# Hymba decoder layer: first weights on the scalar queue, four split buffers, four-quarter openings, later squares on GpSimd

## The reference

```python
u = rms_norm(h, norm_mix);  z = u @ w_in                 # 1024 x 3328
y = concat(rwkv7_time_mix(z[:, :1792]), moba_attention(z[:, 1792:]))
h = h + y @ w_mix_out                                    # 1024 x 1024
h = h + softmax_attention(rms_norm(h) @ w_xq, rms_norm(mem) @ w_xkv) @ w_xo
h = h + square(relu(rms_norm(h) @ w_ff1)) @ w_ff2        # 1024 x 4096 x 1024
out = rms_norm(h, norm_final)
```

## Time and profile before

| | |
|---|---|
| median of 3 runs | 481.69 us (479.34, 481.69, 481.86) |
| profiled execution | 479.82 us, span 477.7 us |
| PE busy | 452.7 us, 95% |
| PEld busy | 404.3 us, 85% |
| DVE busy | 321.8 us, 67% |
| ACT busy | 246.5 us, 52% |
| POOL busy | 35.2 us, 7% |
| from HBM | 71.35 MB, 152 GB/s over the span |

### The profile page before, as it was taken

How to read it: one execution, slowest core, us unless ns; L and a number is a source line. 1 busy time by engine, 2 the same in 40 slices (tenths; PEclk the granted TensorE clock), 3 DMA queues, 4 the chain that set the end, 5 groups by cost and what they waited for, 6 DMA issues and landing times.

```text
span 477.7 us, 10346 instructions
## 1 busy us (share of the span) xinstructions
PE 452.7 (95%) x4390; PEld 404.3 (85%) x4390; DVE 321.8 (67%) x475; ACT 246.5 (52%) x396; POOL 35.2 (7%) x54
## 2 busy tenths in 40 slices
PE   4999999999899999899999997999999999999995
PEld 3999999878788888899998995888888888888883
DVE  3667899985567948569476367575747575666656
ACT  4799944245464446337344344555544354544444
POOL 8300000000000000052000053000000000000000
PEclk9999999999999999999999999999999999999999
DMA  8953464222422415454443155446565746657412
GB/s 247 308 186 114 151 195 149 92 92 80 124 93 89 126 59 170 137 171 159 153 155 111 50 144 160 157 140 231 177 196 161 245 151 217 199 197 230 142 69 88
DMA packets 59937, 73.05 MB, mean 153 GB/s; under 512 B 1378, under 2 KB 48564, under 8 KB 59892
## 3 DMA queue, kind: packets, MB, share of 16 engines
q1 hardware_dynamic: 59812, 72.14, 46.7%
q0 software_dynamic: 80, 0.26, 0.2%
HBM read 71.35 MB, written 1.05 MB: 152 GB/s over the span
## 4 chain that ended last, share of the span: by engine, by line
PE 71%; DVE 12%; ACT 5%; issue 3%; ACTq 0%; DVEq 0%
PE bank L542 9%; PE bank L556 7%; PE bank L558 7%; PE bank L557 7%; PE bank L593 6%; PE bank L595 6%; PE bank L594 6%; PE bank L540 5%; DVE w_lo L1314 4%; DVE op L1403 2%; PE bank L573 2%; ACT w_hi L992 2%; PE bank L575 2%; PE bank L574 2%; PE bank L917 2%
## 5 line engine op out<-in xcount | busy, mean ns | idle before, releaser
L1314 DVE TENSOR_TENSOR w_lo<-raw,w_hi 128x1024 fp32r<-128x1024 f32 x128 | 158.9, 1251 | 76.6 <-ACT w_hi L992 76.3
L992 ACT ACTIVATE w_hi<-raw 128x1024 fp32r<-128x1024 f32 x128 | 133.2, 1054 | 70.1 <-PE bank L558 28.2
L556 PE MATMUL bank<-op,w_hi 128*128 128x256 f32 x416 | 121.4, 292 | 4.5 <-DVE w_lo L1314 2.8
L558 PE MATMUL bank<-op,w_lo 128*128 128x256 f32 x416 | 117.8, 283 | 1.1 <-issue 1.1
L557 PE MATMUL bank<-op,w_hi 128*128 128x256 f32 x416 | 117.6, 283 | 0.0
L556 PEld LDWEIGHTS bank<-op,w_hi 128*128 128x128 f32 x416 | 79.5, 191 | 7.6 <-issue 6.2
L558 PEld LDWEIGHTS bank<-op,w_lo 128*128 128x128 f32 x416 | 79.6, 191 | 1.5 <-issue 1.5
L542 PE MATMUL bank<-op,w_hi 128*128 128x512 f32 x224 | 80.0, 396 | 0.0
L557 PEld LDWEIGHTS bank<-op,w_hi 128*128 128x128 f32 x416 | 79.7, 191 | 0.2
L540 PE MATMUL bank<-op,w_lo 128*128 128x256 f32 x256 | 66.4, 280 | 0.1
L540 PEld LDWEIGHTS bank<-op,w_lo 128*128 128x128 f32 x256 | 48.3, 189 | 2.9 <-DVE op L1403 0.4
(11 more groups left out here) (258 smaller groups left out, 606.4 us busy)
## 6 DMA issues: line engine op xcount, KB each, us to landing
raw<-in_w_ff SPq DMA_DIRECT2D x32, 1024.0 KB, 5.5
raw<-in_w_in SPq DMA_DIRECT2D x12, 1024.0 KB, 5.4
raw<-in_w_xkv SPq DMA_DIRECT2D x8, 1024.0 KB, 5.3
raw<-in_w_mix_out SPq DMA_DIRECT2D x4, 1024.0 KB, 5.0
raw<-in_w_xq SPq DMA_DIRECT2D x4, 1024.0 KB, 5.0
raw<-in_w_xo SPq DMA_DIRECT2D x4, 1024.0 KB, 4.9
xval<-in_x SPq DMA_DIRECT2D x4, 256.0 KB, 4.8
raw<-in_w_in SPq DMA_DIRECT2D x4, 256.0 KB, 5.5
```

Of the source, the lines that this page charges most:

```text
L556: mm(dst, wh[:, k, :], op_hi[which][:, k, :], start=first, stop=False)
L558: last = mm(dst, wl[:, k, :], op_hi[which][:, k, :], start=False, stop=final)
L992: op(view(w_hi), r, ACT.Copy).then_inc(hi_done, 1)
L1314: tt(view(w_lo), r, view(w_hi).bitcast(f32), ALU.subtract).then_inc(lo_done, 1)
```

## The change

Seven things change; no matmul is added or removed.

- The first unit's four DMAs go from SP's queue to ACT's, ahead of all other work of ACT. SP then issues x back to back.
- `NSPLIT` goes from 3 to 4: a split waits for PE to be done with half s-4. The room comes from `tmp`, `rinv` and `center`, which now lie in tensors that are unused at that time (`fresh`, `rinv[1]`, `center` and `hid_sum`).
- The three openings run their four first quarters (0,0) (1,0) (2,0) (3,0), then the four second ones. For mix and xo, halves 0 and 1 of a unit are then open together, so half 1 of units 0 and 1 gets a bank of its own, and DVE takes such a tile in two additions of 256 columns instead of one of 512.
- GpSimd waits for operand j of mix on DVE (`dve_op`) instead of for the addition; after xo it waits for all four operands.
- `rms(2)` on PE stands after quarter 105 instead of after quarter 100 (xq begins at 100), with two quarters instead of six between it and `scores(0)`. `rms(3)` stands eight quarters later, `residual(3)` behind it; `residual(0)` no longer waits for it.
- At the start PE transposes all of x before the first quarter, and ACT runs `stats(0)` before `load(0, 3)`.
- The lists of PE, ACT and DVE are written out anew. Around the mixer's output ACT and DVE make splits 50 and 51 thus: DVE before `operand 1, S50, operand 2, S51, operand 3, S52`, after `operand 1, S50, operand 2, operand 3, S51, S52`; before f1 ACT has S65, S66 and S67 ahead of operand 2 of xo, where before S66 and S67 stood behind it.

```diff
-NRAW, NSPLIT = 3, 3
+NRAW, NSPLIT = 3, 4
...
-        QUARTERS += [(2 * _u + _i, _late ^ _p ^ 1) for _i, _p in
-                     ((0, 0), (2, 0), (0, 1), (1, 0), (1, 1), (2, 1), (3, 0), (3, 1))]
+        QUARTERS += [(2 * _u + _i, _late ^ _p ^ 1) for _p in range(2) for _i in range(4)]
...
+        def half_of_out(o, i):
+
+            what, j = OUTS[o][3:5]
+            if i and j < 2 and what in ("mix", "xo"):
+                return B[{"mix": 4, "xo": 2}[what] + j][:, 0:T]
+            return dense_bank[o % 2][:, i * T:i * T + T]
...
-                sp.dma_start(first_to[:, k, :], first[:, k, UNITS[0][3]:UNITS[0][3] + 256]).then_inc(first_in[i], 16)
...
-                    pool.wait_ge(out_taken, FIRST[what] + j + 1)
+                    if what == "mix":
+                        pool.wait_ge(dve_op, op_no("mix", j) + 1)
+                    elif j == 0:
+                        pool.wait_ge(dve_op, op_no("xo", 3) + 1)
...
+            for i in range(4):
+                k = slice(2 * i, 2 * i + 2)
+                act.dma_start(first_to[:, k, :], first[:, k, UNITS[0][3]:UNITS[0][3] + 256]).then_inc(first_in[i], 16)
             act.wait_ge(pool_const, 1)
...
-            params(0); load(0, 0); load(0, 1); load(0, 2); dense(1); load(0, 3); dense(2); params(1); dense(1)
+            params(0); load(0, 0); load(0, 1); load(0, 2); load(0, 3); dense(4); params(1); spread(0); dense(8)
...
+                    if j < 2:
+                        tt(h[:, 0, :], half_of_out(o, 0), h[:, 0, :], ALU.add)
+                        tt(h[:, 1, :], half_of_out(o, 1), h[:, 1, :], ALU.add).then_inc(out_taken, 1)
+                        return
```

More of the change, by code:

```diff
@@ L957, in _ @@
+            pair_turn(3, 1); dense(1); states_out(); dense(2); deviation(); pair_values(3); gate(); dense(30)
+            rms(2); dense(2); scores(0); dense(2); scores(1); turn(0); dense(2); values(0); dense(1); turn(1)
+            scores(2); dense(2); values(1); dense(1); turn(2); scores(3); dense(2); values(2); turn(3); dense(1)
+            values(3); dense(13)
             dense(4)
-            rms(3)
-            for i in range(4):
+            for i in range(3):
                 dense(2)
@@ L961, in _ @@
                 residual(i)
+            dense(2)
+            rms(3)
+            dense(2)
+            residual(3)
             dense(len(QUARTERS) - at[0])
@@ L1277, in _ @@
-            split(); operand('mix', 3); split(); rms(2); split(); split(); scores(0); split(); split(); turn(0)
-            scores(1); split(); split(); values(0); turn(1); scores(2); split(); values(1); turn(2); split()
-            scores(3); values(2); turn(3); values(3); split(); split(); split(); split(); follow(29); follow(30)
-            split(); follow(31); split(); split()
+            load(0, 0); load(0, 1); load(0, 2); stats(0); load(0, 3); split(); copies(0); split(); follow(0)
+            split(); copies(1); split(); split(); stats(1); follow(1); gates(); split(); split(); follow(2)
@@ new lines, in _ @@
+            pair_turn(3, 1); split(); head_root(); pair_values(3); split(); split(); gate(0); gate(1); split()
+            split(); split(); split(); split(); split(); operand('mix', 0); split(); operand('mix', 1)
+            operand('mix', 2); operand('mix', 3); split(); split(); split(); rms(2); split(); split(); split()
+            scores(0); turn(0); scores(1); values(0); split(); split(); turn(1); scores(2); split(); values(1)
+            split(); split(); turn(2); scores(3); values(2); turn(3); values(3); split(); split(); follow(29)
@@ L1281, in _ @@
+            split(); split(); follow(30); split(); split(); follow(31)
             at[0] = PHASE["xo"]
@@ L1283, in _ @@
             rms(3)
-            for i in range(4):
+            for i in range(3):
                 dense(2)
                 residual(i)
+            dense(4)
+            residual(3)
             dense(len(QUARTERS) - at[0])
@@ L1746, in _ @@
-            take(16); split(); states_out(); split(); take(17); split(); take(18); split(); normalize(); gate(0)
-            gate(1); split(); gate_low(0); split(); pair_values(3); take(19); split(); gate_low(1); split()
-            take(20); split(); split(); split(); take(21); take(22); split(); split(); split()
-            operand('mix', 0); take(23); operand('mix', 1); split(); operand('mix', 2); split()
-            operand('mix', 3); split(); take(24); take(25); split(); split(); scores(0); take(26); weigh(0)
@@ new lines, in _ @@
+            spread_copy(1); keys(0); split(); take(4); keys(1); split(); split(); keys(2); follow(4); take(5)
+            split(); follow(5); split(); take(6); keys(3); split(); tails(0); tails(1); reads(); weighted()
+            load(1, 0); tokens(); follow(6); split(); take(7); bonus(); split(); split(); split(); load(1, 1)
+            mats(0); masked(0); split(); take(8); mats(1); invert(0); invert(1); invert(2); masked(1); invert(3)
+            invert(4); take(9); invert(5); split(); invert(6); take(10); load(1, 2); load(1, 3); join()
@@ new lines, in _ @@
+            take(15); split(); split(); take(16); pair_values(2); state(3); pair_mask(3, 0); pair_mask(3, 1)
+            scale(4); state(4); scale(5); pair_share(3, 0); state(5); pair_share(3, 1); split(); scale(6)
+            state(6); split(); take(17); states_out(); split(); split(); split(); take(18); normalize()
+            pair_values(3); gate(0); take(19); split(); gate(1); split(); gate_low(0); gate_low(1); split()
+            take(20); split(); split(); take(21); split(); split(); take(22); split(); operand('mix', 0)
@@ new lines, in _ @@
+            take(23); operand('mix', 1); split(); operand('mix', 2); operand('mix', 3); split(); split()
+            take(24); split(); take(25); split(); scores(0); take(26); weigh(0); split(); scores(1); split()
+            weigh(1); take(27); values(0); split(); scores(2); weigh(2); split(); values(1); take(28); split()
+            scores(3); weigh(3); split(); split(); values(2); values(3); split(); take(29); take(30); split()
+            split(); follow(29); split(); take(31); split(); follow(30); split(); follow(31); take(32)
```

116 lines of the change are left out of this document (51 added, 65 removed).

## The result

The changed kernel takes 476.89 us in the median of 20 runs (474.59 to 481.61), the kernel before 481.15 us (479.34 to 484.01, 20 runs): ratio 0.9928, 95% interval 0.9902 to 0.9954. The ratio is that of the means (477.66 and 481.13), so 3.5 us less; the medians are 4.3 us apart. Forecast were 6.0 us less. The profiled execution went from 479.8 to 476.1 us, its span from 477.7 to 474.4.

The account below looks back on a forecast made before the run. PE was taken as the bound, busy 452.7 of 477.7 us, so only its waits could be won. Terms summed to -5.0 us, and -1.0 for waits at 0.2 made -6.0: median 481.69 to 475.7, range 471.5 to 480.7.

Parts of the forecast that it names:

- xq: Stage after mix: GpSimd's squares slow DVE's operands 2 and 3 and split 51, a loss of 1.5 us, bounds -0.8 and +2.4.
- xo: Opening of xo: the late operand has one more early quarter ahead of it, -0.7 us, bounds 0 and -1.0.
- z stage: Stage after the start: four split buffers and new lists remove two w_lo waits, -0.8 us, bounds 0 and -1.1.
- f1: Opening of f1: splits 66 and 67 stand ahead and GpSimd's squares come later, -2.6 us, bounds 0 and -3.2.
- The 7.7 us of waits that name an engine: PE's listed waits on another engine from the first full unit on; waits on issue were set aside.
- The start: Up to the first full unit: weights on ACT's queue let it begin at 18.8 instead of 19.94 us, -1.1 us.
- DVE by 16.2: At the start: with x there at 9.3 us, DVE finishes its share, split 2 included, by about 16.2 us.
- two waits at 0.2: Each PE wait costs some 0.2 us more than it shows; two such waits are counted in the stage.
- Attention stage: Attention: waits there are mostly on issue, which the change doesn't affect, so 0 us; bounds +2 and -0.7.
- Mix opening: Opening of mix: pair_values(3) before the gates and four early quarters remove its waits, -1.3 us, bounds 0 and -1.3.
- GpSimd's squares set both stages: Rival, chance 0.08: the squares' 6.4 us on DVE fall on PE in full after mix and in f1; 486.0 us.
- The waits move: Rival, chance 0.14: new lists hold up later splits; if attention gives back 5 us, only the start's gain remains, 480.6 us.

Follow-up runs that it names:

- e1: Changed kernel with the first unit's four DMAs back on SP's queue, alternating with x: 476.96 us, ratio 0.9906.
- e5: Kernel before with only the fourth split buffer and the tensors moved to make room; old lists, openings, queues and squares: 475.88 us, ratio 0.9893.
- e6: Changed kernel with the lists of PE, ACT and DVE between quarters 36 and 79 as in the kernel before: 475.27 us, ratio 0.988.
- e8: Changed kernel with 64 already met waits at the head of PE's stream: 486.28 us, ratio 1.0091.
- e2: Changed kernel with GpSimd's squares after mix waiting for DVE's addition, as before: 474.54 us, ratio 0.9873.
- e3: Changed kernel with GpSimd's squares after xo waiting for the additions, as before: 481.97 us, ratio 0.9985.
- e7: Changed kernel with split 51 ahead of operand 3 of mix in DVE's list: 478.49 us, ratio 0.9943.
- e4: Changed kernel with GpSimd's squares after mix behind all four operands: 478.76 us, ratio 0.9953.

## Why the prediction was right, and where it was off

The median, 476.89 us, lay in the range, 1.2 us above the forecast; the gain by the ratio, 3.5 us, is 2.5 short of the 6.0. Mix, xq and xo came out in size and for the causes given, the start and z stage gave a little less, f1 more, and what is short is one stage put at nothing. The 7.7 us of waits that name an engine leave out 0.7 us at L768, 0.4 at L593, 0.3 at L917 and 0.2 at L656; the same places have 2.1 us in the changed kernel. By its steps:

**The start, forecast -1.1, measured -0.5.** The transfers went as forecast: quarter 0 at 10.24 us (forecast 10.1). The first unit's matmuls were over at 17.2 (forecast 17.9), which is luck: the spacing went from 0.213 to 0.12 us at 12.7 and not at 14.6, so 11 matmuls ran at the lower level and not 21, and PE had then worked without a pause since 8.6. What failed is "DVE by 16.2" for split 2. In the new order PE transposes the parameters after the fourth quarter instead of after the third, and DVE's `params(1)` stands ahead of split 2:

```profile
17.49 0.23 DVE L1453 COPY par<-bank 128x74 f32<-128x74 f32 x1 [0.91 <-PE bank L638]
...
18.04 1.23 DVE L1335 TENSOR_TENSOR w_lo<-raw,w_hi 128x1024 fp32r<-128x1024 f32 x1
```

```profile
18.15 0.68 PE L667 MATMUL bank<-prob,ones 128*128 128x128 f32 x4 [0.70 <-DVE one_k_a L1457]
19.41 0.36 PE L566 MATMUL bank<-op,w_hi 128*128 128x256 f32 x1 [0.58 <-DVE w_lo L1335]
```

I counted 0.9 us from the last matmul of the first unit to the first full unit; it took 2.2. The queue itself gave 1.1 at quarter 0 and 0.8 to 1.7 at the first full unit (e1), the whole term; the order took about 1.0 of it back.

**z stage, forecast -0.8 and two waits at 0.2, measured -1.1.** Right in size. The cause I named, the buffer, is not it alone: with the buffer and the old lists nothing is won there (e5).

**Attention stage, forecast 0, measured +2.5, in five other executions +1.35 to +2.2 and in a sixth +6.4.** This is the step that failed; of its bounds, +2 and -0.7, the upper was too low as well. The stage wasn't quiet: each engine's list is new, and PE's waits on issue grew by 3.4 us, in the others by 1.6 to 4.5. "The change does nothing for them" was wrong: e6 and e8 show that they hang on the order and on the place of the instructions in PE's stream. In the changed kernel:

```profile
83.54 0.43 PE L748 MATMUL bank<-AR,s 64*32 64x64 f32 x24
85.95 1.25 PE L748 MATMUL bank<-AR,s 64*32 64x64 f32 x104 [1.99 <-issue]
...
139.54 0.39 PE L568 MATMUL bank<-op,w_lo 128*128 128x256 f32 x1 [1.82 <-issue]
```

The first wait falls within one group of 128 small matmuls, the second between two matmuls of one quarter, so no semaphore is in it. What ends them is in the last section; why this order makes them larger isn't shown.

**Mix opening, forecast -1.7 with the two waits' 0.2, measured -1.5.** PE goes from the last matmul of quarter 79 (191.82) to the first of mix (192.06) without a wait, and no split is late. The place of `pair_values(3)` is 1.0 of it: with the old lists that wait is back (e6).

**xq, forecast +1.5 and two waits at 0.2, so +1.9; measured +2.2** up to quarter 108, of which the squares are 1.75 (e2), at the places written down. The size of the waits is right by two errors that cancel: they came at nearly full price, 2.3 us of the 2.4, and the old 0.8, which was to stay, went. Answering to the earlier trace rows, DVE and GpSimd in the changed kernel:

```profile
218.98 1.21 DVE L1335 TENSOR_TENSOR w_lo<-raw,w_hi 128x1024 fp32r<-128x1024 f32 x1
220.12 4.28 DVE L1428 SCALAR_TENSOR_TENSOR op<-hT,par,op 128x256 fp32r<-128x256 f32 x4
224.32 4.28 DVE L1335 TENSOR_TENSOR w_lo<-raw,w_hi 128x1024 fp32r<-128x1024 f32 x2
```

```profile
217.35 1.03 POOL L469 TENSOR_TENSOR s<-hT 128x512 f32<-128x512 f32 x1 [90.88 <-DVE op L1428]
219.21 1.89 POOL L471 TENSOR_TENSOR s<-hT 128x512 f32<-128x512 f32 x1 [0.82 <-DVE op L1428]
221.17 1.36 POOL L472 TENSOR_TENSOR s<-s 128x512 f32<-128x512 f32 x1
```

Operands 2 and 3 take 4.28 us instead of 1.75, splits 51 and 52 the same instead of 2.4; split 50, begun at 218.98, took its 1.21 us, and it was GpSimd's square, begun 0.2 us behind it, that took 1.89 instead of 1.03. So the old wait of 0.8 is gone, and the new ones are fuller than the two thirds I took. PE waits for operand 3 and then for split 51, in this order:

```profile
222.87 0.39 PE L566 MATMUL bank<-op,w_hi 128*128 128x256 f32 x1 [0.35 <-DVE op L1428]
...
224.45 0.39 PE L566 MATMUL bank<-op,w_hi 128*128 128x256 f32 x1 [0.60 <-DVE op L1428]
...
226.76 0.36 PE L566 MATMUL bank<-op,w_hi 128*128 128x256 f32 x1 [1.34 <-DVE w_lo L1335]
```

The other 0.5 us, which e2 has too, is in part its wait for the split (1.1 us, before 0.8) and in part the norm's: `rms(2)` stands two quarters ahead of the scores instead of six, and the first scores wait 0.2 us for the scaled query (L928), which they didn't before. I had asked whether the squares are done for `rms(2)`, and not what comes between it and the scores.

**xo, forecast -0.9, measured -1.0.** The operand's wait is gone from the list.

**f1, forecast -3.0, measured -3.9** up to quarter 160. No wait above 0.3 us is left at L547; the 0.6 that I left for split 69 didn't come, and some further time was won in the first f2 units. Of the causes I gave, the squares' place weighs 3.1 us (e3). But the buffer alone, with the squares in the old place, wins 3.4 us in the same stage (e5), so the two don't add up. My reading is that the four-quarter opening wants its fourth split early, and with GpSimd on DVE it comes late; e3's wait of 2.0 us before the fourth quarter fits it. Whether the opening in two quarters with late squares would do as well or better wasn't tried.

**The rivals.** That GpSimd's squares set both stages did not come about in f1, where DVE had the time; the price that the prediction took from the Trainium skill (SBUF — State Buffer, "Who interferes with whom"), all of GpSimd's time on DVE, is not what DVE paid: the four operand instructions of 1.75 us took 2.53 more, while GpSimd was busy for some 3.7 us of that time. By that rule whoever comes second waits, so GpSimd can pay too, and the trace agrees: its square, begun 0.2 us behind DVE's split, took 1.89 us instead of 1.03. "The waits move" describes a part of what happened: 1.35 to 2.5 us in the attention stage, and 6.4 once. Against the rule of the Trainium skill (DMA: Bandwidth & Descriptors, "Issuing engines are not separate DMA queues") that a second issuing engine saves only sequencer time, usually small beside the transfer, e1 shows 1.1 us at quarter 0, of the 1.5 us by which the fourth part of x is issued earlier: the rule's reason holds, its "small" doesn't for a start of eight transfers of 256 KB.

## What to carry to other kernels

Look at what "issue" waits do in a stage before calling it untouched: an order written anew can cost more there than the waits that it removes on operands. When work of GpSimd is moved because it slows DVE, count DVE's time at the new place with the same prices; it paid before f1, where the operands got free, and lost before xq, where it landed on them. And try the resource alone: the fourth buffer without any new order gave as much as the whole change, and with two of its parts undone the kernel is 7.2 us faster than before, where the changed one is 3.5 and 5.0 us faster in its two measurements. Profile the changed kernel twice before you give a stage's loss a size: here one stage alone differed by 1.2 us between two executions of the same program, while all later ones agreed within 0.03.

## What the runs showed of the hardware

**Waits on issue.** They come among PE's small matmuls and in the dense quarters just behind them, move when instructions are put in front, and reach 3.7 us (e8). Each trace has 35 packets of 16 KB of an instruction queue. In the changed kernel one starts at 83.46 us, just ahead of the wait from 84.0 to 85.95, and one at 137.14, ahead of that from 137.7 to 139.54. It is so everywhere: in the fourteen traces there are 31 waits on issue of 1 us or more after the start, and each ends 2.2 to 3.1 us after such a packet starts: 2.8 us or more where the packet took 1.4 to 2.0 us, 2.6 or less where it took 0.9 to 1.2. Most packets have no wait behind them; the kernel before has one at the same 83.47 us and none there. So the waits end with a fetch of instructions, and that PE has run out of them is my reading; no run changed the fetches by themselves.

**They can cost more than they last.** In e7, whose lists differ from the changed kernel's in one DVE swap after mix, a wait on issue of 2.0 us stood in `join`, where the other unpadded kernels had none:

```profile
107.23 0.92 PE L779 MATMUL bank<-neu 32*32 32x32 f32 x69 [2.00 <-issue]
```

and the granted clock (the sixth figure after the busy times, here 0.77) fell in the stretch around it:

```profile
105.00:110.00 5.00, 3.00 (x104) 2.19 (x92) 0.92 (x2) 0.00 (x0) 0.00 (x0) 0.77 0.02 3
110.00:115.00 5.00, 5.00 (x119) 4.29 (x122) 3.16 (x7) 1.94 (x4) 0.00 (x0) 0.89 0.01 3
```

A part of it ran at the lower level, 1.2 GHz, and quarter 48 starts 4.6 us later than in the changed kernel for 2.0 us of wait. By the end of quarter 79 it is 3.7 us later, of the 5.8 by which this execution's span is above the changed kernel's; the other 2.1 were lost at xq in the same way. The wait of 3.5 us for the squares in e4 and the three largest waits of e8 did the same. The length of a wait alone doesn't settle it: the wait of 2.0 us in the changed kernel, at 84 us, left the clock at 1.00, and in e4 it fell behind a wait of only 0.6, to 0.87 from 120 to 125 us and 0.79 from 125 to 130. The runs of the changed kernel vary in the same way: 474.8 and 476.1 us at a mean granted clock of 0.999, 480.6 to 481.6 at 0.985 and 0.986. A profiled execution at 0.999 therefore shows a kernel of this kind at its best, and a comparison of two profiles can miss a microsecond or more that the medians have.
